# Sums of squares over a head's rows: one fp32 product with the block matrix becomes two rounded ones

## The reference, cut to what matters

```python
def rms_norm(x, g):
    xf = x.astype(jnp.float32)
    y = xf * lax.rsqrt(jnp.mean(xf * xf, axis=-1, keepdims=True) + EPS)
    return (y * g.astype(jnp.float32)).astype(x.dtype)

# even layer: 8 query heads and 2 key heads of kind a, 8 and 8 of kind b
aq = apply_rope(rms_norm(aq.reshape(b, s, A_Q_HEADS, HEAD_DIM), a_qn), cos, sin)
ak = apply_rope(rms_norm(ak.reshape(b, s, A_KV_HEADS, HEAD_DIM), a_kn), cos, sin)
bq = rms_norm(bq.reshape(b, s, B_HEADS, HEAD_DIM), b_qn)
bk = rms_norm(bk.reshape(b, s, B_HEADS, HEAD_DIM), b_kn)
# odd layer: 16 query and 16 key heads
q = rms_norm(q.reshape(b, s, C_HEADS, 2, HEAD_DIM), qn)
k = rms_norm(k.reshape(b, s, C_HEADS, 2, HEAD_DIM), kn)
```

## Time and profile before

| | |
|---|---|
| median of 3 executions | 2003.43 us (2001.92 to 2003.45) |
| the profiled execution | 2000.55 us, its span 1998.7 us |
| TensorE | 1934.7 us busy, 97% |
| VectorE | 1043.1 us, 52% |
| ScalarE | 995.8 us, 50% |
| GpSimd | 948.8 us, 47% |
| the chain that ended last | TensorE 79%, VectorE 12%, ScalarE 3% |

### The profile page before, as it was taken

How to read it: one execution, slowest core, us unless ns; L and a number is a source line. 1 busy time by engine, 2 the same in 40 slices (tenths; PEclk the granted TensorE clock), 3 DMA queues, 4 the chain that set the end, 5 groups by cost and what they waited for, 6 DMA issues and landing times.

```text
span 1998.7 us, 26979 instructions
## 1 busy us (share of the span) xinstructions
PE 1934.7 (97%) x10040; PEld 1609.2 (81%) x10040; DVE 1043.1 (52%) x1942; ACT 995.8 (50%) x1743; POOL 948.8 (47%) x1236
## 2 busy tenths in 40 slices
PE   6999999999999999999999999999999999999997
PEld 5778887777778777777788888888879888888886
DVE  4366546566543677766737554412546574444214
ACT  5465735666644555556427444422655364444323
POOL 4542355555544444443454555555452445555552
PEclk9999999999999999999999999999999999999999
DMA  5321123222322222222132222233221222223232
GB/s 189 96 67 43 64 79 91 76 77 75 90 74 85 74 75 74 74 74 74 64 105 84 99 98 95 92 99 94 84 66 53 85 67 103 95 98 101 90 94 71
DMA packets 55203, 169.38 MB, mean 85 GB/s; under 512 B 7073, under 2 KB 13857, under 8 KB 54945
## 3 DMA queue, kind: packets, MB, share of 16 engines
q1 hardware_dynamic: 54784, 166.92, 26.1%
q10 hardware_dynamic: 288, 0.74, 0.1%
HBM read 158.72 MB, written 2.10 MB: 80 GB/s over the span
## 4 chain that ended last, share of the span: by engine, by line
PE 79%; DVE 12%; ACT 3%; issue 2%; POOL 2%; DMA 1%; SPq 0%; ACTq 0%; DVEq 0%; POOLq 0%
PE ps L1843 20%; PE ps L1846 20%; PE ps L1844 20%; PE ps L1903 3%; PE ps L1888 3%; PE ps L1855 2%; PE ps L1858 2%; PE ps L1856 2%; PE ps L1896 1%; DVE tmp L2396 1%; POOL wl L2571 1%; DVE s_xbc L2375 1%; PE ps L1877 1%; DVE s_st L2412 1%; DVE tmp L2419 1%
## 5 line engine op out<-in xcount | busy, mean ns | idle before, releaser
L2571 POOL TENSOR_TENSOR wl<-st,wh 128x256 fp32r<-128x256 f32 (+1 forms) x1180 | 880.5, 778 | 1000.4 <-ACT wh L2009 999.9
L1843 PE MATMUL ps<-xh,wh 128*128 128x512 f32 x1432 | 584.8, 408 | 3.5 <-DVE tmp L2263 3.5
L1846 PE MATMUL ps<-xh,wl 128*128 128x512 f32 x1432 | 559.2, 390 | 0.0
L1844 PE MATMUL ps<-xl,wh 128*128 128x512 f32 x1432 | 558.2, 390 | 0.0
L2009 ACT ACTIVATE wh<-st 128x1024 fp32r<-128x1024 f32 (+2 forms) x311 | 313.9, 1011 | 486.3 <-PE ps L1846 446.1
L1843 PEld LDWEIGHTS ps<-xh,wh 128*128 128x128 f32 x1432 | 269.4, 188 | 64.2 <-issue 10.4
L1846 PEld LDWEIGHTS ps<-xh,wl 128*128 128x128 f32 x1432 | 268.7, 188 | 57.9
L1844 PEld LDWEIGHTS ps<-xl,wh 128*128 128x128 f32 x1432 | 269.6, 188 | 54.2 <-issue 4.8
L2530 DVE SCALAR_TENSOR_TENSOR tmp<-ps,vec,tmp 128x510 f32<-128x510 f32 (+1 forms) x176 | 131.3, 749 | 209.1 <-ACT tmp L2188 206.2
L2488 DVE SCALAR_TENSOR_TENSOR res<-res,ps 128x512 f32<-128x512 f32 (+1 forms) x37 | 22.7, 615 | 220.6 <-PE ps L1846 211.9
L1843 PE MATMUL ps<-fa_h,wh 128*128 128x512 f32 x308 | 120.6, 392 | 0.0
(11 more groups left out here) (276 smaller groups left out, 3407.5 us busy)
## 6 DMA issues: line engine op xcount, KB each, us to landing
st<-in_f_up SPq DMA_DIRECT2D x88, 512.0 KB, 3.2
st<-in_o_fm SPq DMA_DIRECT2D x32, 512.0 KB, 3.6
st<-in_s_xbc SPq DMA_DIRECT2D x32, 512.0 KB, 3.5
st<-in_f_dn SPq DMA_DIRECT2D x32, 512.0 KB, 3.5
st<-in_e_fm SPq DMA_DIRECT2D x21, 512.0 KB, 3.6
st<-in_s_z SPq DMA_DIRECT2D x16, 512.0 KB, 3.5
st<-in_s_out SPq DMA_DIRECT2D x16, 512.0 KB, 3.4
tmp<-tmp SPq DMA_DIRECT2D x100, 64.0 KB, 2.0
```

Of the source, the lines that this page charges most:

```text
L1843: e.matmul(u.bank.ap, hi, x.h[:, kk, :], start=first, stop=False)
L1844: e.matmul(u.bank.ap, hi, x.l[:, kk, :], start=False, stop=False)
L1846: e.matmul(u.bank.ap, lo, x.h[:, kk, :], start=False, stop=last).then_inc(S["mm"], 1)
L2571: e.tensor_tensor(P.mem["wl"][w.m % NWR][:, part], P.mem["stage"][w.m % NSTAGE][:, part], P.mem["wh"][w.m % NWR][:, part].bitcast(F32), AL ...
```

## The change

`qk_prep_g` squares the unit as before, squares it a second time into a rounded tile (`qsq_hi`, ScalarE), subtracts the rounded from the exact squares in place (`qsq_lo`, VectorE), and sums the two parts by two fp32r products into the same bank (`blk`). The block matrix gets a rounded copy, made once by ScalarE at the start of the program from `const` (`blk_r`). Scratch tiles get a second name of type fp32r at the same address; each preparation holds one scratch tile more until `blk` has ended. In the table of costs `blk` goes from 857 to 454, and `blk_r` is given 205; the two other new steps have their engine's default (620 on ScalarE, 692 on VectorE).

```diff
-LENGTHS = {"mm": 681, "mm_half": 362, "mm_tok": 681, "ones": 857, "blk": 857, "turn0": 2000, "turn1": 2000, "cumsum": 960, "bc_t": 330, "dt_t": 270,
+LENGTHS = {"mm": 681, "mm_half": 362, "mm_tok": 681, "ones": 857, "blk": 454, "blk_r": 205, "turn0": 2000, "turn1": 2000, "cumsum": 960, "bc_t": 330, "dt_t": 270,
...
+        for s, rounded in zip(self.tmp.slots, mem["tmp_r"]):
+            s.rounded = rounded
...
         s = yield from self.taken(self.tmp)
         a = yield ("qsq", s, u)
+        hi = yield from self.taken(self.tmp)
+        b = yield ("qsq_hi", hi.rounded, u, hi.freed)
+        b2 = yield ("qsq_lo", s.rounded, s.ap, hi.rounded.bitcast(F32), [a, b])
         st = yield from self.taken(self.aux)
         r = yield from self.taken(self.tmp)
-        t = yield ("blk", st, s, a)
+        t = yield ("blk", st, hi.rounded, s.rounded, [b, b2, self.blk_ready])
         s.release(t)
+        hi.release(t)
...
     P.put("table", "natural_log_exp_and_others", [])
     x = Acts(H, L, 8)
+    P.blk_ready = [P.put("blk_r", mem["blk_r"], P.c(C_BLK), P.pload)]
...
         elif kind == "blk":
-            st, s, squared = o
+            st, hi, lo, squared = o
             pe.freed(st)
             pe.wait_ge(squared)
-            e.matmul(st.ap, P.c(C_BLK), s.ap, start=True, stop=True).then_inc(S["blk"], 1)
+            e.matmul(st.ap, P.mem["blk_r"], hi, start=True, stop=False)
+            e.matmul(st.ap, P.mem["blk_r"], lo, start=False, stop=True).then_inc(S["blk"], 1)
...
+        elif kind == "blk_r":
+            out, src, loaded = o
+            act.wait_ge(loaded)
+            e.activation(out, src, ACT.Copy).then_inc(S["blk_r"], 1)
+        elif kind == "qsq_hi":
+            hi, u, freed = o
+            act.wait_ge(u.done)
+            act.wait_ge(freed)
+            e.activation(hi, u.bank.ap, ACT.Square).then_inc(S["qsq_hi"], 1)
...
+        elif kind == "qsq_lo":
+            lo, src, hi, rounded = o
+            dve.wait_ge(rounded)
+            e.tensor_tensor(lo, src, hi, ALU.subtract).then_inc(S["qsq_lo"], 1)
...
+        mem["blk_r"] = at("blk_r", TMP + 2 * K * nt + 512, [128, 128], F32R)
+        mem["tmp_r"] = [at(f"tmp_r{i}", TMP + 2 * K * (i + 2), [128, 512], F32R) for i in range(nt - 2)]
```

More of the change, by code:

```diff
@@ L64 @@
             "dt_e", "dt_ln", "a_exp", "ct_hi", "sel", "wend_e", "gsq", "gln", "grs", "msq", "ln_out", "ln_hi", "csq",
-            "f0", "fsilu", "sine", "lat", "q_in", "v_a", "head_hi", "gate_in", "gate_s"),
-    "dve": ("nrm", "split_lo", "v_in", "va_out", "bias_s", "bias_m", "neg_sink", "neg_g", "qk_n", "rope_add",
+            "f0", "fsilu", "sine", "lat", "q_in", "v_a", "head_hi", "blk_r", "qsq_hi", "gate_in", "gate_s"),
+    "dve": ("nrm", "split_lo", "v_in", "va_out", "bias_s", "bias_m", "neg_sink", "neg_g", "qk_n", "qsq_lo", "rope_add",
             "mask", "add_b", "mn", "sink_mn", "flip_d", "sink_x", "sums", "rec", "o_n", "y_g", "res_add", "acc",
@@ L100, in __init__ @@
     def __init__(self, ap):
-        self.ap, self.freed, self.idle = ap, [], True
+        self.ap, self.freed, self.idle, self.rounded = ap, [], True, None
 class Use:
@@ L108, in __init__ @@
         self.slot, self.ap, self.freed, self.ready = slot, slot.ap, slot.freed, []
+        self.rounded = slot.rounded
         slot.freed, slot.idle = [], False
```

## The result

The kernel with the change takes **2006.1 us** (median of 21 runs, 2003.57 to 2007.1); the kernel before, run beside it, 2002.81 (21 runs, 2000.45 to 2004.49). The ratio is 1.0015, 95% interval 1.0008 to 1.0021: about 3 us slower where 8.5 less was forecast. The profiled execution took 2006.41 us, its span 2004.6.

A forecast was written before the change was run, and what follows sets the result against it. TensorE, busy 97% of the span, was taken as the bound. Products -12.1, chain in front +2.6, chain behind 0, start +1.0 sum to -8.5 us: 1994.9 us median, range 1989.0 to 2000.5.

The forecast's parts named there:

- Time taken off TensorE's queue in these stretches should shorten the kernel: Two attention layers: TensorE, busy 245 of 250 and 285 of 300 us, bounds them, unless a new wait fills the gap.
- The product term: 29 block products in the attention layers: 0.87 us each replaced by pairs of 0.45, -12.1 us in all.
- The chain in front: Ahead of the block product: second square and subtraction lengthen 0.6 to 1.9 us; TensorE's waits grow by 2.6 us.
- Elsewhere ... nothing: 29 squares and subtractions, 17 us of ScalarE and 20 of VectorE, cost nothing beyond the waits; some 40% is spare.
- The chain behind: From block product to end of `qk_n`, holding the PSUM bank: no change in waits, 0, bounds -2 and +4.
- Start: Program start: rounded block matrix heads ScalarE's queue and waits for `vec`; first projection 1.0 us later, bounds 0.4 and 1.6.
- Rival 2: VectorE's subtraction and GpSimd delay each other at the shared port: +7 us, 2002; chance 0.13 with part of its price.
- Rival 3: Units hold the PSUM bank 0.9 us longer, each preparation puts it on the path: +27 us, 2030; chance 0.06.
- Rival 1: Both layers' new order halves old TensorE waits for the preparation and `o_pr`: -14 us, 1989; chance 0.15.
- Rival 4: Block product: a switch of operands or weights makes the pair cost 0.87 us after all, 2007; chance 0.03.
- Rival 5: Granted clock: the fall at 1618 us is lost (-3) or another caught (+3); chance 0.03, several together included.

The follow-up runs named there:

- pair_keep: Kernel before, its order kept, with the block product as an fp32r pair reading one rounded square twice, block matrix rounded on GpSimd: 2000.62 us, ratio 0.9988.
- hi_keep: Kernel before, its order kept, with one fp32r block product of one rounded square, block matrix rounded on GpSimd: 2002.31 us, ratio 0.9992.
- order_old: Order planned for the change with the work of before: fp32 block product, no second square, no subtraction; block matrix rounded on GpSimd: 2009.35 us, ratio 1.0031.
- order_pair: Order planned for the change, pair reading one rounded square twice, no second square or subtraction; block matrix rounded on GpSimd: 1999.98 us, ratio 0.9984.
- blkr_pool: The whole change, with only the rounded block matrix made on GpSimd instead of ScalarE: 2005.2 us, ratio 1.0011 to the kernel before.
- blkr_rope: The whole change, block matrix rounded on GpSimd, with GpSimd's rotary products cut from 512 to 128 columns: 1994.69 us, ratio 0.9964 to the kernel before.

## Why the prediction was wrong

- *"Time taken off TensorE's queue in these stretches should shorten the kernel"*: this is the step that failed. The size of the pair was right (0.45), its worth wasn't. In the order of before 12 us less of TensorE's work are worth 2.4 us (pair_keep), 18.7 are worth no more (hi_keep). A busy share of 95 to 98% had convinced me. But a record of a product is 0.39 us long and its slot 0.226, so each gap shows 0.16 us shorter than it is, as the section on the time before says itself. I read the chain of waits over the whole span only; over 300 to 590 us alone it shows the projections at 38% and TensorE near a half.
- *The product term*, -12.1: in the order of the change it is worth 9.4 (order_old against order_pair; 7.0 between their two profiled runs).
- *The order*: I gave a new order no price of its own. With the work of before it costs 3 to 6 us (order_old), with the pair nothing, which I hadn't thought of at all; nor had I seen that the plan moves six copies to ScalarE. Term missing.
- *The chain in front, +2.6*: the waits of TensorE for the subtraction are 3.5 us, where about 5 were forecast and 2.6 stood before. As a measure of what the two steps cost they were wrong: they cost 5.2 (order_pair to blkr_pool), 4.4 by the step on VectorE alone, and by blkr_rope, where such waits are 1.4 us and the cost is 5.4, not through these waits.
- *"Elsewhere ... nothing"*: the sentence that VectorE and ScalarE have 40% to spare was right for ScalarE (0.7 us for 29 squares) and wrong for VectorE. Its idle time is waiting for TensorE, ScalarE and GpSimd in a fixed order, and a step put between two of its waits delays all that follow.
- *The chain behind, 0*: TensorE's waits for `qk_n` are 2.0 us in the odd layer, 3.5 before. In its bounds.
- *Start, +1.0*: the first square began at 8.36 instead of 5.79 and the first projection came 1.1 us later, as forecast; at the first unit this trace is 2.4 behind. blkr_pool shows 0.9 us in the medians. The late squares are shown; the size is about 1, and neither the traces (which spread by up to 2.4 us here) nor the medians resolve it.
- Rival 2 (VectorE and GpSimd) was the nearest: its place, 1.75 us instead of 0.69 beside GpSimd, is what the trace shows at 376 us, and the Trainium skill's rule ("SBUF — State Buffer", "Who interferes with whom") agrees with all three rows above: with one input in PSUM the spread is gone. But it put the cost into the waits of the pair, at +7 in all, and took -8.5 as its base. Contention lengthened the subtractions by 5.4 us in all (25.3 against 19.9), and the runs give it some 2 us of the time, with intervals that overlap. Rival 3 (extra time in each preparation eats the gain) was right in kind, wrong in place and size: it is VectorE's queue more than the bank, and 5.2 us in all, 0.18 per preparation, are enough where the pair is worth less than 12.
- Rival 1 fell: the waits for `o_pr` by VectorE's line are 5.0 us, 5.1 before. Rival 4 is excluded by the pair's 0.45. Rival 5: the trace of after has two falls more and, like before, the one near 1620 us; they add up to 3.4 us, and by the mean clock of all runs to 2.6 at most, but don't sort the kernels.

In medians, as differences to before by the ratios: the order with the old work +6.2, the pair -9.4, the second square and the subtraction +5.4, the copy on ScalarE +0.8, together +3.0. The parts were measured one after the other in this sequence; since the pair is worth less in the other order, they aren't independent prices: by the other route the pair is -2.4 (pair_keep), the new order then -0.8 (order_pair), and the rest as above. Not settled: how much of the 5.4 is contention, which step of VectorE's queue is the one that carries the delay on from place to place, and what bounds the odd layer once GpSimd is relieved.

## What to carry to other kernels

Before pricing work taken off the busiest engine, take the chain of waits over the very stretch in which it is taken, and let one cheap run leave that work out with the order kept: here it would have shown 2.4 of 12 us. Work on an engine that is half idle is free only if nothing queued behind it is waited for; price it by the chain behind it, not by the wait for its own result. With a planner, a changed cost is a change of its own: run the new order with the old work, and a split that pays in one layer only can be left to that layer.

## What was unexpected of the hardware

The same VectorE subtraction took 0.67 to 1.75 us beside GpSimd with two inputs in SBUF, and 0.67 to 0.69 with one of them in PSUM (29 instances each); yet removing the spread bought only some 2 us, in a plan that was not quite the same. Cutting 21 pairs of rotary products in the two layers, on an engine that is 47% busy, brought 11.5 us there, by its own queue or by VectorE's sum, which fell from 1.16 to 0.69 us; 12 us less of work on TensorE, 97% busy, brought 2.4.
